# Seven half-size products for the output projections and the sparse queries, each sparse product read by VectorE behind its copy of the second turned group

## What is computed

```python
# first block, twice (two layers); the context tokens take part in the first layer alone
x = x + gate * (concat(mla, gqa, conv) * silu(gates)) @ w_out[l]      # 1280 x 1024 @ 1024 x 1024, then 1024 x 1024 @ 1024 x 1024
# second block: sparse attention with 16 heads of 128 latent channels
q_b = (x @ w_dq).reshape(B, L, 16, 128)                               # the sparse queries
o_b = dsa_attention(q_b, c_kv, mask of the 256 best keys)             # softmax(q_b @ c_kv.T / sqrt(128)) @ c_kv
y_b = (o_b @ w_uv) @ w_dsa_proj
mixed = (sigmoid(gate_a) * y_a + sigmoid(gate_b) * y_b) @ w_out_2
```

## Time and profile before

| | us |
|---|---|
| median of 3 runs | 4604.38 |
| lowest and highest | 4603.16, 4605.92 |
| profiled execution, device time | 4607.54 |
| its span, first to last instruction | 4605.4 |
| TensorE busy in the span | 4440.0 |
| VectorE, ScalarE busy | 2448.4, 1274.5 |
| mean granted TensorE clock, share of full | 0.988 |

### The profile page before, as it was taken

One profiled execution on the slowest core, in us unless ns is written; L12 is line 12 of the kernel. 1 busy time (PEld: TensorE's weight loads), 2 busy tenths in 40 slices (PEclk: granted clock), 3 DMA queues, 4 the chain that ended last, 5 costly groups with the idle time before them and its releaser, 6 DMA issues.

```text
span 4605.4 us, 47360 instructions
## 1 busy us (share of the span) xinstructions
PE 4440.0 (96%) x19380; PEld 2445.6 (53%) x19380; DVE 2448.4 (53%) x4138; ACT 1274.5 (28%) x2014; POOL 51.9 (1%) x74
## 2 busy tenths in 40 slices
PE   7998999999998999999999999999999999999997
PEld 3554667845444678544457645555544444444443
DVE  6677556723576567228952313333443555656554
ACT  2004445512015455213023403333300311110033
POOL 1000000000000000000000000000000000000000
PEclk9999999999999999999999999999999999999998
DMA  7212000021120000200110010000012211111112
GB/s 276 80 60 87 1 1 1 2 105 60 44 92 20 1 1 2 81 28 23 37 41 28 19 37 19 19 15 14 28 46 64 64 46 46 37 46 64 46 51 69
DMA packets 49463, 207.18 MB, mean 45 GB/s; under 512 B 4897, under 2 KB 4897, under 8 KB 46689
## 3 DMA queue, kind: packets, MB, share of 16 engines
q1 hardware_dynamic: 36512, 142.62, 9.2%
q0 software_dynamic: 12736, 61.54, 3.5%
HBM read 185.27 MB, written 18.87 MB: 44 GB/s over the span
## 4 chain that ended last, share of the span: by engine, by line
PE 92%; DVE 4%; ACT 2%; DMA 1%; issue 1%; POOL 0%; ACTq 0%; DVEq 0%; PEld 0%; PEldq 0%; SPq 0%; POOLq 0%
PE psum L2429 20%; PE psum L696 9%; PE psum L1243 7%; PE psum L1448 5%; PE psum L1281 5%; PE psum L2109 5%; PE psum L1262 5%; PE psum L1700 5%; PE psum L392 3%; PE psum L2383 3%; PE psum L1813 2%; PE psum L1803 2%; PE psum L2395 2%; PE psum L2125 2%; PE psum L1840 2%; PE psum L705 1%
## 5 line engine op out<-in xcount | busy, mean ns | idle before, releaser
L2429 PE MATMUL psum<-arena 128*128 128x512 f32 x2184 | 937.8, 592 | 1.0 <-DVEq L375 1.0
L2429 PEld LDWEIGHTS psum<-arena 128*128 128x128 f32 x2184 | 414.8, 190 | 523.2 <-issue 521.8
L696 PE MATMUL psum<-arena 128*128 128x512 f32 x952 | 410.0, 592 | 0.0
L2734 DVE TENSOR_TENSOR arena<-arena,psum 128x512 f32<-128x512 f32 x280 | 192.3, 687 | 397.2 <-PE psum L2429 388.6
L1243 PE MATMUL psum<-arena 64*128 64x256 f32 (+2 forms) x1584 | 386.3, 443 | 6.8 <-ACT arena L1196 5.8
L696 PEld LDWEIGHTS psum<-arena 128*128 128x128 f32 x952 | 180.9, 190 | 223.8 <-issue 222.2
L1262 PEld LDWEIGHTS psum<-arena 128*128 128x128 f32 x1968 | 226.8, 141 | 133.9 <-issue 110.4
L1319 ACT ACTIVATE arena<-psum,arena 128x1280 f32<-128x1280 f32 (+1 forms) x216 | 265.9, 1241 | 112.5 <-DVE arena L1350 107.4
L1262 PE MATMUL psum<-arena 128*128 128x128 f32 x1968 | 278.2, 276 | 10.8 <-DVE arena L1383 5.5
L1448 PE MATMUL psum<-arena 128*128 128x512 f32 (+1 forms) x640 | 248.3, 550 | 2.0 <-PEq L375 2.0
L1324 ACT ACTIVATE arena<-psum 128x512 f32<-128x512 f32 x294 | 164.8, 597 | 294.7 <-PE psum L1262 294.7
(11 more groups left out here) (297 smaller groups left out, 5262.2 us busy)
## 6 DMA issues: line engine op xcount, KB each, us to landing
arena<-stream SPq DMA_DIRECT2D x228, 512.0 KB, 3.6
arena<-mod_t POOLq DMA_DIRECT2D x32, 512.0 KB, 4.5
arena<-mod_w POOLq DMA_DIRECT2D x4, 2048.0 KB, 25.9
arena<-stream SPq DMA_DIRECT2D x6, 1024.0 KB, 9.4
arena<-x SPq DMA_DIRECT2D x4, 1280.0 KB, 16.3
gated<-arena POOLq DMA_DIRECT2D x4, 1280.0 KB, 4.7
arena<-gated SPq DMA_DIRECT2D x1, 5120.0 KB, 16.1
arena<-x POOLq DMA_DIRECT2D x2, 2048.0 KB, 19.8
```

The lines of the kernel that those rows point to most:

```text
L696: last = nc.tensor.matmul(ps(PROJECT_BANKS[p], 512), lhsT=lhsT(k), rhs=rhs(k), start=k == 0, stop=k == 3)
L2429: last = nc.tensor.matmul(ps(pair_bank(j, p), HALF), lhsT=lhsT(k), rhs=rhs(k), start=k == 0, stop=k == nk - 1)
L2734: step(nc.vector.tensor_tensor(out, a, b, op), ev)
```

## The change

Three things change together.

1. Output projection: the 8 blocks become 4 pairs of blocks for each column chunk, and each pair is made by seven products of four matmul calls over half the chunk (256 columns, 128 in the last chunk of layer 0). VectorE makes 4 data sums for each chunk and 4 weight sums for each pair (in the first chunk only). Products 1, 6, 7 and 4 of a pair pile up in one bank, and ScalarE copies that bank out behind products 1, 6 and 7; products 5 and 3 pile up in another. VectorE adds three parts and writes four half-chunk results to the residual.
2. Sparse queries: the four query units of a pair become seven products of four calls over 512 columns, one behind the values of each of steps 0 to 6, all in BANK6. The value units stand behind steps 1 and 2. VectorE makes four weight sums (two in step 0, one in step 1, one in step 2) ahead of its copy of group 1, and reads each product one step later, behind its copy of group 1 and ahead of `top`. Group 2 of the transposes has BANK6 too and waits for that read. ScalarE no longer copies query units.
3. For the data sums of the queries, `MIX_AT` is emptied: four DMAs of 1 MB on GpSimd's queue store the mixed tiles, four more bring them back during the tail. The sums of `x` are made at the start of the sparse attention and used by the first group of the tail too.

```diff
+    OUT_BLOCKS = [OUT_W_AT + 6 * 1024 + i * 1024 for i in range(7)] + [TAB_AT + T + i * 1024 for i in range(3)] + [OUT_SUM_AT + 1024 + i * 1024 for i in range(3)]
...
+    def out_bank(q, p):
+
+        return (q % 2 * 3 + {1: 0, 6: 0, 7: 0, 4: 0, 2: 1, 5: 2, 3: 2}[p]) * 512
...
     def pe_outproj(t, l):
...
+        for q in range(n_pairs):
+            t.eng.wait_ge(out_copied.sem, OUT_COPIED[l, q, 1])
+            weights_summed(q, 2)
+            data_summed(q, 2)
+            product(q, 6, ws(q, 2), ys(q, 2))
+            product(q, 5, ws(q, 1), ys(q, 1), first=True)
+            t.eng.wait_ge(out_copied.sem, OUT_COPIED[l, q, 6])
+            weights_summed(q, 3)
+            data_summed(q, 3)
+            product(q, 7, ws(q, 3), ys(q, 3))
+            if q + 1 < n_pairs:
+                first_product(q + 1)
+            t.eng.wait_ge(out_copied.sem, OUT_COPIED[l, q, 7])
+            data_summed(q, 4)
+            product(q, 4, w(q, 1, 1), ys(q, 4))
+            if q + 1 < n_pairs:
+                second_product(q + 1)
+            if q >= OUT_PAIRS and q % OUT_PAIRS == 0:
+                pe_norm_sum(t, l, q // OUT_PAIRS - 1)
+            t.eng.wait_ge(out_read.sem, out_read_count(l, q, C22))
+            weights_summed(q, 4)
+            product(q, 3, ws(q, 4), y(q, 1, 1))
...
     def act_outproj(t, l):
...
+        copy(0, 1)
+        for q in range(n_pairs):
+            copy(q, 6)
+            copy(q, 7)
+            if q + 1 < n_pairs:
+                copy(q + 1, 1)
+            if q:
+                squares(q - 1)
+            v, j = divmod(q, OUT_PAIRS)
+            if v and j == 1:
+                root(v - 1)
+            if v:
+                for k in NORM_SLOTS.get(j, ()):
+                    affine(v - 1, k)
+        squares(n_pairs - 1)
...
     def dve_outproj(t, l):
...
+        data_sum(0, 1)
+        data_sum(0, 2)
+        weight_sum(0, 1)
+        weight_sum(0, 2)
+        data_sum(0, 3)
+        weight_sum(0, 3)
+        data_sum(0, 4)
+        weight_sum(0, 4)
+        for q in range(n_pairs):
+            v, j = divmod(q, OUT_PAIRS)
+            part(q, 0, 2, 1)
+            if q + 1 < OUT_PAIRS:
+                for i in range(1, 5):
+                    weight_sum(q + 1, i)
...
+            part(q, 2, 5, 7)
...
+            if q:
+                adds(q - 1)
...
+            if v and j == 1:
+                variance(v - 1)
+            if v:
+                for k in NORM_SLOTS.get(j, ()):
+                    scale(v - 1, k)
+            part(q, 1, 3, 6)
+            outputs(q)
+        adds(n_pairs - 1)
...
     def pe_dsa(t):
...
+        def product(p, r):
+            g, n = BLOCKS["dsa"] + 2 * p, 7 * (p - 1) + r
+            if n:
+                t.eng.wait_ge(product_read.sem, SPARSE_READS + n)
...
+            for k in range(4):
+                last = nc.tensor.matmul(ps(BANK6, HALF), lhsT=lhsT(k), rhs=rhs(k), start=k == 0, stop=k == 3)
...
         def turn(u, g, tiles):
             j = SPARSE_STEPS[u][1]
             if g == 3:
                 t.eng.wait_ge(sparse_moved[1].sem, t.next(sparse_moved[1]))
+            if g == 2 and products[0]:
+                t.eng.wait_ge(product_read.sem, SPARSE_READS + products[0])
...
             values(u)
-            if p + 1 < DH // 2 and 1 <= u % 8 <= 6:
-                unit(6 * (p + 1) + u % 8 - 1)
+            if p + 1 < DH // 2:
+                if u % 8 < 7:
+                    product(p + 1, u % 8)
+                if 1 <= u % 8 <= 2:
+                    value_unit(p + 1, u % 8 - 1)
...
     def dve_dsa(t):
...
+        def read(p, r):
+            t.eng.wait_ge(product_done.sem, SPARSE_PRODUCTS + 7 * (p - 1) + r + 1)
...
+            if r == 0:
+                step(nc.vector.tensor_scalar(c21, ps(BANK6, HALF), -DL ** -0.5, None, ALU.mult), product_read)
+            elif r == 5:
+                add(c22, c22, dve_step)
+                add(c12, c12)
+            else:
+                add(*{1: (c11, c21), 2: (c12, c21), 3: (c22, c12), 4: (c21, c22), 6: (c12, c12)}[r])
+
+        t.eng.wait_ge(stored.sem, 16 * (4 * LAYERS + STORED_PAIRS))
+        b11, b12, b21, b22 = (data_quarter(0, h, v) for h in range(2) for v in range(2))
+        sums = [data_sum(0, i, 4) for i in range(4)]
+        for sum_out, a, b in ((sums[0], b12, b11), (sums[1], b22, sums[0]), (sums[2], b22, b12), (sums[3], b21, sums[1])):
+            step(nc.vector.tensor_tensor(sum_out, a, b, ALU.subtract), data_sums)
...
             scales(u)
+            if p + 1 < DH // 2:
+                for i in {0: (1, 2), 1: (3,), 2: (4,)}.get(u % 8, ()):
+                    weight_sum(p + 1, i)
             if len(groups) > 1:
                 move(1, groups[1])
+            if p + 1 < DH // 2 and u % 8:
+                read(p + 1, u % 8 - 1)
             if u + 1 < len(SPARSE_STEPS):
                 top(u + 1, 0)
...
     def dve_tail(t):
...
-        data_sums_of(0, 1)
-        weight_sum(0, 3, True)
-        weight_sum(0, 1, True)
-        data_sums_of(0, 2)
-        weight_sum(0, 2, True)
-        data_sums_of(0, 3)
-        data_sums_of(0, 4)
-        weight_sum(0, 4, True)
+        for i in (3, 1, 2, 4):
+            weight_sum(0, i, True)
...
     @block.gpsimd
...
+        for i in range(STORED_PAIRS):
+            t.eng.wait_ge(mixed_done.sem, t.next(mixed_done))
+            eng.dma_start(io["gated"][:, 2 * i * T:2 * (i + 1) * T], sb(MIX_AT + 2 * i * T, 2 * T)).then_inc(stored.sem, 16)
+        t.eng.wait_ge(stored.sem, t.next(stored, STORED_PAIRS))
+        t.eng.wait_ge(product_done.sem, PRODUCTS + 7 * (KD // 2 - 1) + P5)
+        for _, m, _ in PAIRS[KD // 2:MIX_PAIRS]:
+            eng.dma_start(sb(MIX_AT + 2 * m * T, 2 * T), io["gated"][:, 2 * m * T:2 * (m + 1) * T]).then_inc(mix_in.sem, 16)
+            t.eng.wait_ge(mix_in.sem, t.next(mix_in))
```

More of the change, by code:

```diff
@@ L1418, in out_weight, with out_loaded @@
     def out_weight(l, m):
         return W_AT + (BLOCKS[f"out{l}"] + m) % 2 * 1024 if m < 2 else OUT_W_AT + (m - 2) * 1024
-    def out_bank(q):
-        return q % 6 * 512
+    def out_loaded(l, m):
+        if m >= 2:
+            return sp_in[m // 2 - 1], 16 * (l + 2)
+        slot, n = (BLOCKS[f"out{l}"] + m) % 2, 0
+        for l2 in range(l + 1):
+            last = PROJECT_BLOCKS + (2 if l2 < l else m + 1)
+            n += sum((BLOCKS[f"proj{l2}"] + i) % 2 == slot and not (i < PROJECT_BLOCKS and in_temporary(l2, i)) for i in range(last))
+        return w_loaded[slot], 16 * n
@@ new lines, in program, with out_sum_counts @@
+    OUT_PRODUCT, OUT_COPIED = out_counts()
+    def out_sum_counts():
+        weight, data, n = {}, {}, 0
+        for l in range(LAYERS):
+            for kind, i in (("d", 1), ("d", 2), ("w", 1), ("w", 2), ("d", 3), ("w", 3), ("d", 4), ("w", 4)):
+                n += 1
+                (weight if kind == "w" else data)[l, 0, i] = n
+            for q in range(out_pairs(l)):
+                if q + 1 < OUT_PAIRS:
+                    for i in range(1, 5):
+                        n += 1
+                        weight[l, q + 1, i] = n
+                if q % OUT_PAIRS == OUT_PAIRS - 1 and q + 1 < out_pairs(l):
+                    for i in range(1, 5):
+                        n += 1
+                        data[l, q // OUT_PAIRS + 1, i] = n
+        return weight, data
@@ new lines, in product, with w @@
+        def product(q, p, lhsT, rhs, first=False):
+            h = out_run(l, q)[1] // 2
+            for k in range(4):
+                ins = nc.tensor.matmul(ps(out_bank(q, p), h), lhsT=lhsT(k), rhs=rhs(k), start=first and k == 0, stop=k == 3, skip_group_check=not first)
+                if k < 2 and p == 3 and out_last(l) == q // OUT_PAIRS:
+                    ins.then_inc(block_done[(g + k) % 2].sem, 1)
+            ins.then_inc(out_product.sem, 1)
+        def w(q, s, half):
+            return lambda k: sb(out_weight(l, 2 * (q % OUT_PAIRS) + s) + (4 * half + k) * P, P)
@@ new lines, in data_summed, with first_product @@
+        def data_summed(q, i):
+            if q % OUT_PAIRS == 0:
+                t.eng.wait_ge(out_sum.sem, OUT_DATA_SUM[l, q // OUT_PAIRS, i])
+        def first_product(q):
+            if q < OUT_PAIRS:
+                for s in range(2):
+                    ev, value = out_loaded(l, 2 * q + s)
+                    t.eng.wait_ge(ev.sem, value)
+                    if ev in w_loaded:
+                        t.next(ev)
+            if q >= 2:
+                t.eng.wait_ge(out_read.sem, out_read_count(l, q - 2, C21))
+            product(q, 1, w(q, 0, 0), y(q, 0, 0), first=True)
@@ L1518, in affine, with copy, squares @@
                     .then_inc(ln_done.sem, 1)
-        for v, (c0, n) in enumerate(cols):
-            for m in range(KD):
+        def copy(q, p):
+            n = cols[q // OUT_PAIRS][1] // 2
+            t.eng.wait_ge(out_product.sem, OUT_PRODUCT[l, q, p])
+            if q >= 2 and p == 1:
+                t.eng.wait_ge(x_new.sem, KD * (l * len(chunks(TC))) + 2 * (q - 1))
```

(21 more changed lines are left out.)

254 lines of the change are left out of this document (182 added, 72 removed).

## The result

The changed kernel takes 4616.94 us (median of 20 runs, 4606.89 to 4623.29) where the kernel before takes 4605.84 beside it (20 runs, 4603.16 to 4608.96): 1.0022 times as long, 95% interval 1.0015 to 1.0029, so 11 us slower. The forecast was 4624.3 in a range of 4603 to 4648, slower the likeliest. Of all runs in this document one, of out_only, was disturbed (4742 us at a granted clock of 0.942) and is left out.

The account below looks back on a forecast made before the run. TensorE's own work was taken as the bound (busy 96% of the span). Terms -21.3 + 27.5 + 14 - 0.3 = +19.9 on the profiled 4607.5 give 4627.4, less 3.2 to the median 4624.3; range 4603 to 4648.

Parts of the forecast that it names:

- term -21.3: Output projections of both layers: TensorE work saved less idle added, -21.3 us in sum, bounds -27 and -8.
- terms +27.5 and the clock: Sparse attention: -24.0 us of work and +51.5 of idle make +27.5; lost clock, partly in the output projections, adds 14.
- TensorE has nothing between groups 1 and 2: Sparse steps 2, 4, 6: transposes run as one stretch, so waits for VectorE's read lie bare, 5.15 us a pair.
- the rival on bare weight loads: Output projections: a quarter of each weight load not hidden behind 256-column records, 43 us more, 4667; chance 0.01.
- Sparse idle, +51.5 foretold: Sparse attention, seven pairs: TensorE waits for VectorE's reads and sums in steps 0, 2, 4 and 6, +51.5 us.
- Sparse work, -24.0 foretold: Sparse queries: four units become seven products, 3.43 us less TensorE work in each of 7 pairs, -24.0 us.
- six in ten at 1.55: 16 x 0.6 x 1.55, about +15: Sparse steps 0, 6 and output projections: six in ten long idles lose 1.55 us to 1.2 GHz; 14 taken, bounds 0 and +25.
- the likeliest case: Whole kernel: the forecast with the clock falling behind idles, 4624.3 us, between 4614 and 4645; chance 0.56.
- the clock holds: Whole kernel: short idles never bring a 1.2 GHz stretch, +5.9 us, 4610, between 4603 and 4616; chance 0.23.
- become the bound in the output projections: VectorE's chain presses on the result bank's release, 1 us in each of 20 pairs, sparse late reads grow; 4650 to 4660; chance 0.12.
- VectorE comes early: Sparse steps 2, 4 and 6: their idle goes, 4574, or about 4590 to 4595 with half the idle; chance 0.07.
- The tail: Tail after the sparse attention: eight sums shrink to four, TensorE hardly waited for them, -0.3 us.

Follow-up runs that it names:

- out_only: Kernel before with only the output projections made by seven products, nothing of the sparse stage; 4584.28 us, ratio 0.9953 to the kernel before.
- sparse_only: Kernel before with only the sparse queries by seven products and the stored mix, on the old output projection; 4633.80 us, ratio 1.0059 to the kernel before.
- read_first: Changed kernel with VectorE reading each product ahead of its copy of group 1, in every step; 4579.68 us, ratio 0.9941 to the kernel before.
- fill_idle: Changed kernel with useless 128-column matmuls in TensorE's idle times of steps 0, 2, 4 and 6, pairs 1 to 6; 4610.51 us, ratio 1.0011 to the kernel before.
- mixed_stored: Kernel before with item 3 alone (mixed tiles stored and reloaded, early data sums); 4606.85 us, ratio 1.0001 to the kernel before.
- sums_late: Changed kernel with the sparse queries' weight sums one step later, none ahead of step 0's copy; 4607.06 us, ratio 1.0003 to the kernel before.
- longer_pair: Changed kernel with one useless 512-column matmul call ahead of product 0 of each sparse pair; 4634.22 us, ratio 1.0058 to the kernel before.
- read_first_sums_late: Changed kernel with both edits: reads ahead of the copy of group 1, and weight sums one step later; 4562.07 us, ratio 0.9909 to the kernel before.

## Why the prediction was right

**Direction, order of size and mechanism held.** The halves alone are -21.8 (term -21.3) and +27.7 (terms +27.5 and the clock). That the second is so near is in part luck: without the falls of the clock the sparse stage is 23 us longer than before in the changed kernel's trace and 24 in sparse_only's, where 27.5 was worked out, and the falls make up for the rest. "TensorE has nothing between groups 1 and 2" is what the idles of 1.45, 1.38 and 2.11 us show, and read_first takes exactly those away.

**Output projections.** Layer 0 saved 10.0 (10.9 foretold): 14.4 of work, where 15.6 was worked out, against 4.5 more idle, where 4.7 was. That idle has the places that were named (the profile's long ones in layer 0; the last of them stood there before too, at 3.39):

```profile
1048.86 3.84 PE L1517 MATMUL psum<-arena 128*128 128x128 f32 x32 [1.75 <-ACT arena L1655]
...
1071.55 1.16 PE L1517 MATMUL psum<-arena 128*128 128x128 f32 x8 [1.04 <-ACT arena L1655]
...
1078.29 5.05 PE L1601 MATMUL psum<-arena 128*128 128x512 f32 x8 [3.17 <-ACT arena L1647]
```

Layer 1 saved 8.4 (10.4 foretold): 11.0 of work, where 13.2 was worked out, against 2.6 more idle, where 2.8 was. Of that 2.04 us stand ahead of the partition sum, close to the 2.3 foretold, and in the profiled execution they are followed by a clock fall. It makes 1.7 of the missing 2.2: in out_only, without it, the same stage saved 10.1, with 12.7 of work. 256-column records stayed at 0.216 us (between the first and last start of 272 in one stretch, 58.95 - 0.36 over 271), so the rival on bare weight loads is out. By the prediction's estimate on the figures of the Trainium skill, "TensorE: Matmul & The Clock Gate", section "Back-to-back issue gap", the projections would have become dearer; out_only is 21.8 us faster, and the measurement decides. No idle stands at the residual's DMA.

**Sparse idle, +51.5 foretold, +46.0 measured.** This term was 5.5 us too high. The sizes of the steps were off by tenths: steps 2, 4 and 6 idle 1.45, 1.38 and 2.11 (4.94 together, 4.6 more than the 0.35 of the earlier trace rows), where 1.1 + 1.6 + 2.4 = 5.1 more was worked out. A read takes 0.68, not the 0.75 taken from the output writes of the earlier trace rows, and starts 0.61 behind the copy. Step 0 idles 2.12 where 0.73 was the earlier trace rows, and 0.54 ahead of group 0: some 1.9 more, against 2.2. Seven pairs of 6.5 give 45.5.

**Sparse work, -24.0 foretold, -19.6 measured** in the window; some 3 us of the difference are the two falls (behind the idles that end at 2772.69 and 2845.94).

**The clock is the term that was mis-sized.** The step "six in ten at 1.55: 16 x 0.6 x 1.55, about +15" gave each idle its own chance. The profiled execution, 2 us below the median, has three falls behind these sixteen idles (two in the sparse stage, one at layer 1's partition sum), where 9.6 were counted on. The falls repeat over the pairs, so that a run can have few of them or many: 16 us between the lowest and the highest run would be some eleven falls at 1.5. The median stands 10 us above the lowest run, where that of the kernel before stands 2.7 above its own: some 7 us of clock, 6 by fill_idle, not 14. The forecast's 4624.3 lies above every one of the 20 runs (the highest is 4623.29): it foretold +19.9, and +11.1 was measured. The clock's term was some 7 us too high and the sparse waits 5.5; the smaller misses of the other terms go both ways. Without the falls the forecast was +5.9; the fastest runs, at 4607 to 4609, are 1 to 3 above the kernel before. So the likeliest case and the rival "the clock holds" (4603 to 4616) are the two ends of one spread, and the median lies near where they meet.

**The other rivals.** VectorE did not become the bound in the output projections, and the sparse stage did not get shorter. "VectorE comes early" is what read_first makes true: 4580, beside the 4574 that it was worked out at. The tail gave -1.9 (-0.3 foretold), about as much as the stretch between the index and the sparse attention lost (+1.7), where TensorE's work is the same as before; mixed_stored shows the DMAs at nothing, as forecast.

## What to carry to other kernels

When a saving on the bounding engine is paid with a wait on an engine that is half idle, look at where in that engine's fixed order the step stands, not at its load: one swap of two statements was worth 37 us here, and the step belongs in the idle time ahead of the copy, not behind it. A bank that two streams share (the product's and group 2's) makes the order of its readers part of the critical path. Where short idles recur in a loop, time many runs before a few microseconds are read as an effect, since the clock may fall behind them in most rounds of one kernel and in few of another.

## What the runs showed that had not been expected

Idles of TensorE of 2.1 us are followed by a stretch at 1.2 GHz or by none, and which of the two it is repeats over the pairs: none of eleven idles in a row in the changed kernel's profile, six pairs in a row in sums_late, every long idle from the second pair's step 6 on in longer_pair, and in read_first two pairs with a fall, one without, and again. Each fall costs 1.3 to 1.6 us and lengthens the pair by as much: sums_late's pairs are 71.8 us long with one fall each, longer_pair's 75.2 with two. The changed kernel's runs spread over 16 us (4606.89 to 4623.29), nearly three times as far as those of the kernel before (5.8 us in 20 runs), and its time follows the granted clock. Not all spread is of these idles, though: read_first_sums_late has no idle of 2 us left in the sparse stage, and its four runs lie 13 us apart (4555.73 to 4568.69, granted clock 0.988 to 0.986). The Trainium skill, on the page named above, section "What's actually happening", says of the matmuls at the low clock at a kernel's start that their number varies from run to run of the same kernel. That the falls inside a kernel vary too agrees with it: the 20 runs' granted clock goes from 0.989 to 0.985. That a loop's length can hold the falls in step no run here proves; what sets the place of the first one stays open.
